# GLA recurrence of a hybrid decoder step: the prompt's query-by-state products as three single-pass products on split parts, in buffers shared with the samples

## What is computed

```python
def step(S, xs):                       # one chunk of T tokens, 4 heads, S: 256 x 512 per head
    qc, kc, vc, gc = xs
    b = jnp.cumsum(gc, axis=2)
    bL = b[:, :, -1:]
    qd = qc * jnp.exp(b)
    A = jnp.einsum('bhtd,bhjd->bhtj', qd, kc * jnp.exp(-b))
    A = jnp.where(causal, A, 0.0)
    o = jnp.einsum('bhtd,bhdv->bhtv', qd, S) + jnp.einsum('bhtj,bhjv->bhtv', A, vc)
    S_new = jnp.exp(bL)[:, :, 0, :, None] * S + jnp.einsum('bhjd,bhjv->bhdv', kc * jnp.exp(bL - b), vc)
    return S_new, o
```

## Time and profile before

| | |
|---|---|
| time, median of 3 runs | 2181.74 us (2181.13 to 2185.22) |
| the profiled execution's own time | 2187.39 us |
| its span | 2185.7 us |
| mean granted TensorE clock | 0.968 |
| TensorE busy | 2051.1 us, 94% |
| VectorE / ScalarE / GpSimd busy | 1324.1 / 843.7 / 275.7 us |
| queries by state, L2714, 32 steps (128 records) | 60.3 us of records, mean 593 ns |

### The profile page before, as it was taken

The page is one execution under the profiler, slowest core; times in us unless marked ns, Lnnn a source line. Parts: engine busy times, 40 slices in busy tenths (PEclk is TensorE's granted clock), DMA queues, the critical chain, the costliest instruction groups (busy, mean ns, idle before and its releaser), DMA issues. The chain is left out here.

```text
span 2185.7 us, 32847 instructions
## 1 busy us (share of the span) xinstructions
PE 2051.1 (94%) x12590; PEld 1841.3 (84%) x12590; DVE 1324.1 (61%) x2299; ACT 843.7 (39%) x1536; POOL 275.7 (13%) x384
## 2 busy tenths in 40 slices
PE   5999999999999589999958999999999699999997
PEld 4999999999999478788738999999999577777774
DVE  5456676555456666666646556655666585666664
ACT  5455543332232444444344444222223344334333
POOL 3000000000000211121121000000000243323322
PEclk8999999999999799999978999999999799999999
DMA  2112133343332645555331322444233444544442
GB/s 101 56 64 63 63 112 90 118 157 94 105 101 79 220 128 165 154 158 164 97 135 44 103 85 80 134 151 128 86 113 100 170 150 166 177 164 171 172 149 69
DMA packets 209222, 264.36 MB, mean 121 GB/s; under 512 B 48228, under 2 KB 156004, under 8 KB 207032
## 3 DMA queue, kind: packets, MB, share of 16 engines
q1 hardware_dynamic: 209080, 262.42, 38.0%
HBM read 172.39 MB, written 89.99 MB: 120 GB/s over the span
## 5 line engine op out<-in xcount | busy, mean ns | idle before, releaser
L547 DVE TENSOR_TENSOR pa_stage<-pa_ps,pa_stage 128x536 f32<-128x536 f32 x110 | 77.0, 712 | 129.9 <-PE pa_ps L514 124.4
L547 DVE TENSOR_TENSOR pc_stage<-pc_ps,pc_stage 128x536 f32<-128x536 f32 x110 | 77.0, 712 | 105.3 <-PE pc_ps L514 93.9
L362 PE MATMUL pa_ps<-a_XT_hi,pa_w_hi 128*128 128x358 f32 x576 | 133.1, 339 | 0.3 <-PEq L197 0.3
L362 PE MATMUL pa_ps<-a_XT_hi,pa_w_lo 128*128 128x358 f32 x576 | 126.0, 327 | 0.0
L362 PE MATMUL pa_ps<-a_XT_lo,pa_w_hi 128*128 128x358 f32 x576 | 125.7, 326 | 0.0
L514 PE MATMUL pc_ps<-c_XT_hi,pc_w_lo 128*128 128x268 f32 x384 | 110.2, 287 | 0.0
L514 PE MATMUL pc_ps<-c_XT_hi,pc_w_hi 128*128 128x268 f32 x384 | 110.2, 287 | 0.0
L514 PE MATMUL pa_ps<-a_XT_hi,pa_w_lo 128*128 128x268 f32 x384 | 110.1, 287 | 0.0
L514 PE MATMUL pc_ps<-c_XT_lo,pc_w_hi 128*128 128x268 f32 x384 | 110.1, 287 | 0.0
L514 PE MATMUL pa_ps<-a_XT_lo,pa_w_hi 128*128 128x268 f32 x384 | 110.1, 287 | 0.0
L514 PE MATMUL pa_ps<-a_XT_hi,pa_w_hi 128*128 128x268 f32 x384 | 109.9, 286 | 0.0
(11 more groups left out here) (542 smaller groups left out, 6153.1 us busy)
## 6 DMA issues: line engine op xcount, KB each, us to landing
pa_w_raw<-in_w_a SPq DMA_DIRECT2D x57, 512.0 KB, 4.6
pc_w_raw<-in_w_c SPq DMA_DIRECT2D x49, 512.0 KB, 4.7
scr_c<-pc_stage SPq DMA_DIRECT2D x48, 512.0 KB, 3.2
scr_a<-pa_stage SPq DMA_DIRECT2D x40, 512.0 KB, 3.2
ma_hin<-scr_a SPq DMA_DIRECT2D x32, 512.0 KB, 3.4
mc_hin<-scr_c SPq DMA_DIRECT2D x32, 512.0 KB, 3.7
mc_sample_state<-in_s SPq DMA_DIRECT2D x32, 512.0 KB, 4.5
out_s_s<-mc_sample_state SPq DMA_DIRECT2D x32, 512.0 KB, 2.9
```

The lines of the kernel that those rows point to most:

```text
L362: ins = pe.matmul(self.ps[:, 3 * s + t, 0:TC], w[:, k, :], x[:, k, t * TC:(t + 1) * TC], start=(k == 0 and j == 0), stop=(k == KT - 1 and ...
L547: dve.tensor_tensor(dst, self.out(p, product), x, ALU.add).then_inc(self.added, 1)
```

## The change

The queries by the prompt's state are no longer two f32 products but six single-pass ones, on split parts of both operands. The queries' parts get buffers of their own, `qh` and `ql`; the state's parts go into `csh` and `csl`, which the sample states use too, in turn: in step n the sample's parts are read in `unit`, then the prompt's parts are written for `part_b(n + 1)`, then the next sample's. ScalarE writes the prompt's high part (`prompt_state_hi`), VectorE the low part (`prompt_state_lo`), GpSimd splits the queries (`split_q`). Unit 0's state is split ahead of the loop; the others' splits stand at the start of the next step instead of the end of this one. The buffer `sc` is dropped: the masked scores are written back to PSUM and split from there.

```diff
+        qh, ql = (a.sb(f"mc_q_{x}", [P, 2, P], F32R) for x in ("hi", "lo"))
-        sc = a.sb("mc_scores", [P, P])
-        csh, csl = (a.sb(f"mc_sample_state_{x}", [P, 2, GV], F32R) for x in ("hi", "lo"))
+        csh, csl = (a.sb(f"mc_split_state_{x}", [P, 2, GV], F32R) for x in ("hi", "lo"))
...
 TensorE, part_b
                     if n >= H:
-                        pe.wait_ge(state_ready, n - H + 1)
+                        pe.wait_ge(prompt_lo_ready, n - H + 1)
+                        pe.wait_ge(q_ready, n - H + 1)
                         for d in range(2):
-                            pe.matmul(ps[0:rows, 3, :], hin[n % 2][:, d, 0:rows], cst[:, h, d, :], start=(d == 0), stop=False)
+                            for j, (q, x) in enumerate(((qh, csh), (qh, csl), (ql, csh))):
+                                ins = pe.matmul(ps[0:rows, 3, :], q[:, d, 0:rows], x[:, d, :], start=(d == 0 and j == 0), stop=False)
+                        ins.then_inc(prompt_read, 1)
...
 ScalarE
 def sample_state_hi(u):
                     if u:
                         act.wait_ge(read_done, u)
+                    if u + 1 >= H:
+                        act.wait_ge(prompt_read, u + 2 - H)
                     act.activation(csh[:], cs[u % SRING][:], ACT.Copy).then_inc(cs_hi_ready, 1)
+
+                def prompt_state_hi(n):
+                    act.wait_ge(state_ready, n - H + 1)
+                    act.wait_ge(read_done, min(n - 1, UNITS))
+                    if n - 1 > UNITS:
+                        act.wait_ge(prompt_read, n - H)
+                    act.activation(csh[:], cst[:, n % H, :, :], ACT.Copy).then_inc(prompt_hi_ready, 1)
...
+                sample_state_hi(0)
                 for n in range(NSTEP):
+                    if 1 < n <= UNITS:
+                        sample_state_hi(n - 1)
                     norm(n)
...
                         stack_hi(item[1], item[2])
+                    if H <= n + 1 < NSTEP:
+                        prompt_state_hi(n + 1)
                     if h == 0 and c:
...
-                    if n < UNITS:
-                        sample_state_hi(n)
...
 VectorE, part_a
-                    dve.tensor_tensor(sc[0:rows, 0:rows], x, mask, ALU.mult).then_inc(sc_chain, 1)
-                    dve.tensor_tensor(sh[0:rows, 0:rows], x, mask, ALU.mult).then_inc(sc_chain, 1)
+                    dve.tensor_tensor(x, x, mask, ALU.mult).then_inc(sc_chain, 1)
                     dve.wait_ge(k_chain, n + 1)
                     dve.tensor_tensor(kl[0:rows, :], k, kh[0:rows, :].bitcast(F32), ALU.subtract)
+                    dve.wait_ge(sc_chain, 2 * n + 1)
+                    dve.tensor_copy(sh[0:rows, 0:rows], x).then_inc(sc_chain, 1)
                     dve.wait_ge(sc_chain, 2 * n + 2)
-                    dve.tensor_tensor(sl[0:rows, 0:rows], sc[0:rows, 0:rows], sh[0:rows, 0:rows].bitcast(F32), ALU.subtract
+                    dve.tensor_tensor(sl[0:rows, 0:rows], x, sh[0:rows, 0:rows].bitcast(F32), ALU.subtract
...
+                def prompt_state_lo(n):
+                    dve.wait_ge(prompt_hi_ready, n - H + 1)
+                    dve.tensor_tensor(csl[:], cst[:, n % H, :, :], csh[:].bitcast(F32), ALU.subtract).then_inc(prompt_lo_ready, 1)
...
+                sample_state_lo(0)
                 for n in range(NSTEP):
+                    if 1 < n <= UNITS:
+                        sample_state_lo(n - 1)
                     add_state(n)
...
                         O.split_w_lo(dve, n)
+                    if H <= n + 1 < NSTEP:
+                        prompt_state_lo(n + 1)
                     if u is not None:
                         update(u)
...
-                    if n < UNITS:
-                        sample_state_lo(n)
...
 GpSimd
+                def split_q(n):
+                    c, h, rows = where(n)
+                    pool.wait_ge(turned, n + 1)
+                    if n > H:
+                        pool.wait_ge(prompt_read, n - H)
+                    q = hin[n % 2][:, 0:2, 0:rows]
+                    pool.tensor_copy(qh[:, :, 0:rows], q).then_inc(qh_ready, 1)
+                    pool.wait_ge(qh_ready, n - H + 1)
+                    pool.tensor_tensor(ql[:, :, 0:rows], q, qh[:, :, 0:rows].bitcast(F32), ALU.subtract).then_inc(q_ready, 1)
...
                     scale_state(n)
+                    if H <= n + 1 < NSTEP:
+                        split_q(n + 1)
                     if n + 1 < NSTEP:
```

More of the change, by code:

```diff
@@ L2560, in stage_mix_c @@
         read_done = sem("mc_sample_read_done")
+        qh_ready = sem("mc_q_hi_ready")
+        q_ready = sem("mc_q_split")
+        prompt_hi_ready = sem("mc_prompt_state_hi_ready")
+        prompt_lo_ready = sem("mc_prompt_state_lo_ready")
+        prompt_read = sem("mc_prompt_state_read")
         os_low = sem("mc_sample_low_copied")
```

## The result

The changed kernel takes **2192.8 us**, median of six runs (2189.54 to 2194.23), beside 2183.78 for the kernel before on the same chips (six runs, 2181.13 to 2185.87). The ratio is 1.0039 with an interval of 1.0026 to 1.0051: slower, by about 8.5 us. The forecast was 2183.6 in a range up to 2192.0; the result is 9.2 above the one and 0.8 above the other. The forecast started from the three runs' 2181.74; 2.0 of the 9.2 us are that start, which six runs put at 2183.78. The profiled execution took 2191.86 us.

What follows compares the result with a forecast made beforehand. TensorE was taken to bound the last stage, its step 12.32 us. Terms -11.0 + 0 + 5.7 + 1.8 + 2.0 + 1.7 + 1.7 = +1.9 us on the 2181.74 median gave 2183.6 us, range 2176 to 2192.

Steps and rivals of the forecast that it cites:

- The products: Query products in 32 steps: six single-pass for two f32 ones save 0.33 to 0.34 us each, -11.0 in all.
- The cover of an ordinary step: Ordinary steps: the added splits on the other engines stay hidden behind TensorE, by a few tenths; extra cost nothing.
- Start: Start of the last stage: products wait 2.6 us, only about 1.2 new, unit 0's split leaves VectorE's queue; booked 0.
- Steps 9 and 17: Where a sample group's keys are prepared: query split delays them, prompt's low part comes late; 2.85 us each, +5.7.
- 10 and 18: Steps after the stalled ones: late `part_m` makes the scores' low part late for the transpose; 0.9 us each, +1.8.
- Steps 5, 13, 21: After a finished chunk: saved 0.34 us is waited out again, plus exposed copy and slip; 0.7 each, +2.0.
- 25 and 29: Steps 25 and 29: VectorE's low part follows `scale_state` and the query split waits it out; 0.85 us each, +1.7.
- 33: Step 33, last chunk: scaling holds back the prompt's low part and then the query split; +1.7 us.
- GpSimd's query split is dear: Rival, GpSimd behind `scale_state`: split takes 2.0 to 2.6 us instead of 1.2; 2189.7 to 2197.2 us, chance 0.25.

Runs made afterwards that it cites:

- Filled: Changed kernel plus 13, 9 and 9 thrown-away single-pass products in TensorE's waits of steps 3, 9 and 17; 2193.59 us, ratio 1.0029 to the kernel before.
- the later kernels that leave these steps alone: Four experiment kernels built on the kernel before, sample-state splits not moved; their steps 0 to 3 take 43.96 to 44.43 us.
- the second run: The changed kernel itself, unedited, run and traced again; ratio 1.0040 (1.0025 to 1.0055) to the kernel before.

## Why the prediction was wrong

It said no change, and the kernel is 0.39% slower. By its steps:

- **The products**, -0.34 each: right but for some hundredths. 1.40 for 1.72, ordinary steps 12.00 to 12.08 for 12.31 to 12.33, and steps 7 to 9 are 0.90 shorter for 1.02. I said 11.95 to 12.0.
- **The cover of an ordinary step**: right. No wait in any of them.
- **"Start ... I book 0, bounds -1.4 and +2.6": this is the step that failed.** Steps 0 to 6 cost 4.0 us more than booked, of an error of 5.5 in the whole stage. The argument was that VectorE's queue would be waited for in the next step anyway, so that only 1.2 of the wait was new. Steps 4 to 6, the part that repeats from run to run, show two misses in it. Booked for them is +0.9: 1.2 of new wait and 0.7 for step 5's turn, less 1.0 of saved products. They cost +5.2. Filled, they cost +2.4, so 2.8 is TensorE's clock: the length of the wait was priced and its effect on the clock was not, 14 products at 0.43. The other 1.5 is mostly the wait itself: it came at 3.12 instead of 2.6, as VectorE and GpSimd held each other up (below), and step 5 gave back 0.8 of it instead of 1.4 (12.00 for 13.15, less 0.34 of saved products). Against this stands the gain of steps 0 to 3: 1.5 us in the changed kernel's trace and 3.0 in the filled one's, which is 1.6 to 2.1 beside the later kernels that leave these steps alone, for the -1.4 of the bound. So the filled kernel's steps 0 to 6, 85.07 for 85.65 in the kernel before and 84.3 to 84.8 in those later ones, come within about 1 us of what I booked, but by errors that partly cancel.
- **Steps 9 and 17, "2.85 us each", and 10 and 18, "0.9 each"**: the waits were 2.21 and 2.20, the lateness behind them larger; filled, steps 10 and 11 together are 3.0 longer than before, for 3.1 booked, and 18 and 19 too. The clock added 1.6 of slow products, half of it hidden in that lateness, and this is what the two pairs cost beyond the sum, 0.7 and 0.6.
- **Steps 5, 13, 21**, 0.7 each: too high. "TensorE already waits 0.36" holds in step 13 alone; in steps 5 and 21 the kernel before has no such wait above 0.1. Steps 6 and 22 grew by 0.22 and 0.19 and step 14 got 0.18 shorter, where +0.36 net was booked for each. **25 and 29**: 0.70 and 0.19 in steps 26 and 30, 0.9 together for 1.0. **33**: 2.1 in step 34 for 1.4, of which about 1.1 is a fall of the clock at 2149.9: with f32 products there, step 34 takes 10.76 with such a fall and 9.70 without. In the second run it was 3.3, and 4.5 more in step 35.
- **The rival "GpSimd's query split is dear"** had the price wrong and the place right. The split costs 0.40 + 0.74 where it runs alone; beside VectorE's work the cast takes up to 1.40 and the subtraction 1.60. The groups of GpSimd's instructions in the last stage (count, busy us, mean ns, idle before):

```profile
L3090 POOL TENSOR_TENSOR mc_q_lo<-mc_hin,mc_q_hi 128x256 fp32r<-128x256 f32 x28 | 21.5, 767 | 2.2
L3088 POOL CAST mc_q_hi<-mc_hin 128x256 fp32r<-128x256 f32 x28 | 14.1, 505 | 0.0
```

1.27 us on average, for 1.2 forecast. But "its place is between `scale_state` and everything else of the step" was the sentence to follow to its end. I priced each step's wait from that place and did not ask whether the place was needed; by the ratios moving it gives back about 10 of the 12.9 us that I had summed as lost in all these steps, though some of that is chance, as said above. In step 3 the change also put it beside the weight splits:

```profile
1769.60 4.28 DVE L1384 TENSOR_TENSOR mc_wout_lo<-wout_c_late,mc_wout_hi 128x1024 fp32r<-128x1024 f32 x3
1770.01 1.60 POOL L3090 TENSOR_TENSOR mc_q_lo<-mc_hin,mc_q_hi 128x256 fp32r<-128x256 f32 x1
```

Three splits in 4.28 us are 1.43 each; where nothing disturbs them two take 2.41. The Trainium skill, "SBUF — State Buffer", section Who interferes with whom, has two-input VectorE operations and GpSimd's reads exclude each other, whoever is first. By that rule, the trace agrees: 0.22 lost on each of VectorE's, and a subtraction of 0.74 that takes 1.60.

The range failed with it. It was built from the bounds of the copies and from the rivals, and none of them had a term for what a wait does to the clock, although it was there to be read in the trace of before: at the stage's start a wait of 1.79 us ends at 1733.95, and from 1735.03 on eight products are slow. The next long one, 1.90 at 1765.98, has no slow product behind it, so that trace alone did not say how often.

## What to carry to other kernels

On an engine that is otherwise never idle, price a new wait of about 2 us or more at its length, and carry 1 to 3 us on top as a risk (it came behind 12 of 16 such waits here, and mostly 0.8 to 2.8 us of it were felt). Look in the trace for a clock below 1.00 behind the waits that are there already. Before work is added to a queue, look for what it needs and for idle time ahead of that queue's own waits: the same two instructions, put in front of the scaling instead of behind it, turned a loss of 0.39% into a gain of 0.09%, which is hardly to be told from none. A change that pays in 28 of 32 steps need not be made in the other four: leaving them out was worth another 0.3%.

## What the runs showed of the hardware

- A wait in the middle of dense work can lower TensorE's clock from 1.00 to 0.50 (2.4 to 1.2 GHz), during the wait or within some 1.5 us of resuming, mostly for 7 to 14 single-pass products of the changed kernel, which costs 1.4 to 2.8 us. Ahead of the query products of the changed kernels all eight waits of 1.95 to 3.12 us had this, and none of seven of 0.70 to 1.62; in the kernel before four of eight of 2.99, and none of four of 0.99 and 1.65. Why fewer there is open. No length divides the two cleanly: at the stage's start, where waits follow each other closely, all nine of 2.78 to 2.80 us ahead of step 2's transposes had it, two of 2.06 and 2.07 didn't, of the 14 of 1.75 to 1.92 ahead of step 3's key products three had it, and of the 14 of 1.44 to 1.79 in step 1 five. The Trainium skill, "TensorE: Matmul & The Clock Gate", section What's actually happening, has the activity looked at on a schedule of its own, which a kernel doesn't restart; that would let equal waits end differently. The runs fit it and don't prove it.
- Products whose result is overwritten keep the clock up: none of the nine filled waits was followed by a slow product. Four of the nine say something, the three of the changed kernel and step 28, since their unfilled twins had slow products; the twins of the other five had none.
- The clock also falls once or twice in the last chunk, where a step has 16 queries, in 13 of the 14 traces, at slightly different places, and in the kernel before as well (at 2165.31). Such a fall costs up to 1.6 us (step 33 takes 15.18 instead of 13.62 in two runs that leave it as before). In the second run of the changed kernel the long one, 2154.6 to 2168.3, begins in the wait of step 33, and there the two can't be kept apart.
